# Differential attention on one Trainium2 core: sixteen value products of a tile split 7 and 9 between two score groups, in place of 3 and 13

## What is computed

```python
def block(args):
    qblk, qp = args                                   # 128 queries
    s = jnp.einsum('bqhce,bkhce->bchqk', qblk, k).astype(jnp.float32) * scale
    dist = jnp.abs(qp[:, None] - pos[None, :]).astype(jnp.float32)
    s = s - slopes[:, None, None] * dist
    a = jax.nn.softmax(s, axis=-1)
    w = a[:, 0] - lam * a[:, 1]
    return jnp.einsum('bhqk,bkhe->bqhe', w.astype(v.dtype), v)
```

## Time and profile before

| | |
|---|---|
| median of 3 runs | 2943.7 us (2941.12 to 2943.79) |
| the profiled execution | 2944.24 us, its span 2942.4 us |
| busy over the span | PE 2735.8 us (93%), PEld 2286.2 (78%), DVE 2032.5 (69%), ACT 1560.2 (53%), POOL 1054.5 (36%) |
| differential attention | 766 to 1296 us of the span |
| mean granted TensorE clock | 0.971 of full speed |

### The profile page before, as it was taken

One profiled execution on the slowest core, in us unless ns is written; L12 is line 12 of the kernel. 1 busy time (PEld: TensorE's weight loads), 2 busy tenths in 40 slices (PEclk: granted clock), 3 DMA queues, 4 the chain that ended last, 5 costly groups with the idle time before them and its releaser, 6 DMA issues. The chain is left out here.

```text
span 2942.4 us, 56410 instructions
## 1 busy us (share of the span) xinstructions
PE 2735.8 (93%) x22114; PEld 2286.2 (78%) x22114; DVE 2032.5 (69%) x2931; ACT 1560.2 (53%) x3111; POOL 1054.5 (36%) x803
## 2 busy tenths in 40 slices
PE   7899989999799999989998899899899999799998
PEld 5678867888588888879998678688677788577776
DVE  5767686666799999967776765433567766466675
ACT  6574446644588888867776221322433333455553
POOL 4677656777122222139550543200021011221211
PEclk9999999999899999999999899999999999799999
DMA  3433322332402120023443666242155466644441
GB/s 115 129 108 94 93 84 88 112 104 86 133 24 60 25 53 24 25 83 99 118 118 101 237 215 253 84 145 79 54 175 131 99 158 159 170 155 135 143 154 69
DMA packets 317445, 330.25 MB, mean 112 GB/s; under 512 B 24400, under 2 KB 259968, under 8 KB 314112
## 3 DMA queue, kind: packets, MB, share of 16 engines
q1 hardware_dynamic: 287184, 292.59, 32.7%
q0 software_dynamic: 6912, 23.07, 2.6%
q10 hardware_dynamic: 23088, 11.02, 1.6%
HBM read 217.13 MB, written 109.47 MB: 111 GB/s over the span
## 5 line engine op out<-in xcount | busy, mean ns | idle before, releaser
L1049 PE MATMUL p_acc<-p_y_hi,p_x_hi 128*128 128x512 f32 x904 | 363.2, 402 | 11.6 <-POOL p_x_lo L562 3.8
L1049 PE MATMUL p_acc<-p_y_lo,p_x_hi 128*128 128x512 f32 x904 | 357.1, 395 | 0.0
L1049 PE MATMUL p_acc<-p_y_hi,p_x_lo 128*128 128x512 f32 x904 | 357.1, 395 | 0.0
L562 POOL TENSOR_TENSOR p_x_lo<-k_carry,p_x_hi 128x1024 fp32r<-128x1024 f32 x113 | 281.9, 2501 | 133.8 <-ACT p_x_hi L634 133.8
L1894 ACT ACTIVATE d_e<-d_e,d_neg_top 128x2048 f32<-128x2048 f32 x128 | 256.8, 2006 | 18.8 <-DVE d_neg_top L1974 18.8
L2061 PEld LDWEIGHTS d_out<-d_v,d_w_t 64*128 64x128 f32 x4096 | 247.8, 188 | 11.9 <-ACT d_a_parts L1909 0.8
L920 DVE RECIPROCAL p_aux<-p_aux 128x512 f32<-128x512 f32 x64 | 215.1, 3361 | 55.8 <-ACT p_aux L730 55.8
L2061 PE MATMUL d_out<-d_v,d_w_t 64*128 64x128 f32 x4096 | 249.4, 272 | 0.7 <-ACT d_a_parts L1909 0.7
L1565 PE MATMUL s_acc<-s_y_hi,s_x_hi 128*128 128x512 f32 x560 | 223.5, 399 | 24.9 <-DVE s_x_lo L1369 13.0
L1565 PE MATMUL s_acc<-s_y_lo,s_x_hi 128*128 128x512 f32 x560 | 220.9, 395 | 0.0
L1565 PE MATMUL s_acc<-s_y_hi,s_x_lo 128*128 128x512 f32 x560 | 220.8, 394 | 0.0
(11 more groups left out here) (364 smaller groups left out, 7187.2 us busy)
## 6 DMA issues: line engine op xcount, KB each, us to landing
k_carry<-in_w_in SPq DMA_DIRECT2D x128, 256.0 KB, 3.3
k_carry<-in_a_w_in POOLq DMA_DIRECT2D x72, 256.0 KB, 3.6
cols<-p_z SPq DMA_DIRECT2D x64, 256.0 KB, 2.6
w_q<-q SPq DMA_DIRECT2D x15, 1024.0 KB, 7.6
o_parts<-l_stage SPq DMA_DIRECT2D x192, 66.0 KB, 1.9
m_o<-o_parts SPq DMA_DIRECT2D x48, 264.0 KB, 5.8
k_carry<-cols SPq DMA_DIRECT2D x48, 256.0 KB, 4.7
j_x_second<-x SPq DMA_DIRECT2D x20, 512.0 KB, 3.8
```

Of the source, the lines that this page charges most:

```text
L562: pool.tensor_tensor(x_lo[:, m % RING], inputs.place(x_place(m)), x_hi[:, m % RING].bitcast(F32), ALU.subtract).then_inc(x_lo_made, 1)
L1049: mm = pe.matmul(bank_of(n, j), x_part[:, n % RING, j, kt], y_part[:, y_slot(n), kt], start=(kt == 0 and m == 0 and not (g == 0 and n % 2 ...
```

## The change

One number in `diff_attention`, used only by TensorE's list:

```diff
@@ -1769,7 +1769,7 @@
             else:
                 eng.wait_ge(k_made, 2 * h)
 
-        EARLY = 3
+        EARLY = 7
         FILLED_AT = (11, 12, 15)
```

## The result

| | before | changed |
|---|---|---|
| median | 2942.41 us (4 runs, 2939.91 to 2943.79) | 2962.84 us (4 runs, 2959.2 to 2964.41) |
| ratio | | 1.0071, 95% interval 1.0056 to 1.0086 |
| profiled execution, span | 2944.24, 2942.4 us | 2962.72, 2960.9 us |

A forecast was written before the change was run, and what follows sets the result against it. The loop through ACT's copy was to bound the stage: 6.27 + 2.03 + 0.11 restart = 8.41 us a unit. Sixty periods +22.3, start -0.4, end -0.9, together +21.0, gave 2964.5 us, range 2955 to 2970.

The forecast's parts named there:

- The loop V, S10, D10, D11, E1, C, V: Per unit: first value product, third score group, DVE's third and fourth reads, second exponential, ACT's output copy, back; 8.41 us.
- S10 to D10: From the start of TensorE's third score group to DVE's third read of scores: 1.12 to 1.13 us.
- C to V: From ACT's copy of the previous unit's output to TensorE's first value product: 0.42 us, from a single sighting.
- D10 to D11: From DVE's third read of a unit's scores to its fourth: 1.40 us.
- The restart: Loss when value products resume after a wait: taken as 0.11 us, with bounds 0 and 0.16.
- V to T0: From the first value product to the first transpose group on TensorE: 1.56 us, or 1.67 with the restart.
- the lower end: Forecast with no loss at the restart of value products: period 8.30 us, total 2958 us.
- S11: TensorE's fourth score group of a unit; its wait for DVE was to be gone or nearly.
- Faster, by a shorter cycle: Rival: copy does not hold value products; TensorE and DVE loop over two units, 7.81 us each, 2929 us; chance 0.06.
- V to S10: From the first value product to the third score group on TensorE: 1.13 us before, 2.03 with the change.
- No change: Rival: the two effects cancel, period 7.95 to 8.15 us, total 2938 to 2949.6 us; chance 0.04.
- Slower still, by the clock: Rival: TensorE's longer idles lower its clock, one unit in ten costing 2.2 us more; 2978 us; chance 0.04.

The follow-up runs named there:

- e3_copy_late: Kernel before the change, with ACT's copy put behind the second pair of moves, no product moved; 2970.81 us, ratio 1.0099 to the kernel before.
- e7_copy_early: Changed kernel with ACT's copy put in front of the same step's second exponential; 2929.07 us, ratio 0.9953 to the kernel before.
- e8_copy_early: As e7_copy_early, but with eight key tiles in front of the first transposes; 2922.55 us, ratio 0.9937 to the kernel before.

## Why the prediction was right

- **The mechanism** was the forecast one. The loop V, S10, D10, D11, E1, C, V, hidden before, grew by the four moved tiles and became the longest. Two runs in which no product is moved switch its cost on and off by the place of the copy: on in the kernel before (e3_copy_late), off in the changed one (e7_copy_early).
- **Its size**: 8.38 in place of 8.41. S10 to D10 took 1.09, not 1.12 to 1.13; C to V took 0.41, not 0.42; D10 to D11 took 1.41, not 1.40. The restart was the unknown; V to T0 took 1.67, so it cost 0.11 as taken, not the 0 of the lower end (1.56).
- **The signs named**: V waiting some 60 times for 35 to 55 us (58 times, 39.3); D10 waiting 0.8 (0.81), S11 nearly none; ACT 1.4 before its moves and 0.2 before E1 (1.44 and 0.24); clock 1.00. All came. TensorE stood 0.66 us before V, where 0.74 were forecast.
- **The start** gained about 0.5 us, as expected: the first mixing comes at 780.07 before and at 779.66 in the changed kernel; with that 0.41 added, the first products of unit 1 come at 798.23 (797.82 in the trace) in place of 798.72.
- **The end** was wrong in sign. I took -0.9 us for the last two units and they cost more than before: from the first product of unit 61 to the last copy 15.2 us (1300.78 to 1315.99), against 14.5 (1281.00 to 1295.53). The step at fault is the one that priced 32 products at 0.1115 there. No scores are left to fill the wait for the copy, so TensorE stood still 2.11 us before unit 61, against 0.65 in the kernel before, and its clock fell (TensorE's timeline, then busy times with the clock in the third column from the end):

```profile
1300.78 2.81 PE L2061 MATMUL d_out<-d_v,d_w_t 64*128 64x128 f32 x28 [2.11 <-ACT d_a_parts L1909]
1303.37 1.07 PE L2044 MATMUL d_turn<-k_ident,d_e 64*128 64x64 f32 x16
```
```profile
1298.00:1301.00 3.00, 0.89 (x24) 0.75 (x22) 2.93 (x5) 2.76 (x6) 0.20 (x1) 1.00 0.00 0
1301.00:1303.00 2.00, 2.00 (x26) 2.00 (x26) 1.99 (x1) 0.70 (x2) 0.25 (x1) 0.60 0.15 41
1303.00:1305.00 2.00, 2.00 (x30) 2.00 (x30) 0.40 (x1) 0.52 (x2) 0.00 (x0) 0.54 0.00 0
```

  V to T0 took 2.59 there, against 1.67 in the loop. From V to T1, unit 61 took 5.80 us (1300.78 to 1306.58) and unit 62, at a clock of 1.00 again, 4.22 (1307.23 to 1311.45). These 1.58 us are the whole miss at the end. They and the 0.03 too much in each of 60 periods (1.8 us) cancelled; that the total came so close is in part luck.
- **A slip of words**: the prediction says that two transposed tiles of the first group stay behind S11. It is one tile, number 7, with its two products. Nothing hung on it.
- **The rivals.** 'Faster, by a shorter cycle' was the right loop for a kernel in which the copy does not hold V, as e7_copy_early and e8_copy_early showed; its condition, V to S10 under 1.68, was not met (2.14). The 1.68 gives a period of 7.95; for the 7.81 of that rival V to S10 would have had to be under 1.54. 'No change' wanted a period of 7.95 to 8.15, and it was 8.38. 'Slower still, by the clock' did not happen in the loop, where TensorE idles 0.66 us a unit at a clock of 1.00, but at the stage's end it did, once. What the Trainium skill says of idles between groups of matmuls (TensorE: Matmul & The Clock Gate, A second HAM failure mode: psum-queue depth-cycling) was so not seen for gaps of 0.66 us. The Trainium skill's advice for the gaps of the most contended engine, to let what blocks it start sooner (Perfetto Trace Analysis, Optimization Strategy), led to a gain here with one tile moved (-13.4 us) and to a loss with four (+20.4).

The stage from the first mixing to the last copy grew by 20.9 us (536.3 against 515.5); the profiled spans differ by 18.5. Of the 2.4 us between them, 0.4 lie ahead of the first mixing and 2.0 behind the last copy. The edit touches nothing there, and executions of one kernel differ by more (2939.91 to 2943.79 us before).

## What to carry over

When work is moved on an in-order engine into a gap, write down the loops that pass through the place it goes to, and not only the one it leaves: the first tile gained 0.22 us a unit, the second lost 0.10 and each of the next two 0.22 to 0.23, because a loop with 0.64 us of slack took over. A single sighting of a wait at the edge of a stage (here 0.42 us, and 0.11 for the restart) can be enough to price a loop that is hidden everywhere else. Before such a split is tuned, see which instruction on another engine closes the loop; putting the copy before a long exponential in place of behind it, together with a new split, gave more than any split alone that was tried. Four to six or more than eight tiles with the copy early were not run, so the best pair is not known.

## What was not expected of the hardware

- **POOL's add and DVE's mixing.** With the copy early, POOL's add of the two halves falls under DVE's mixing of two SBUF inputs (1007.71 to 1010.06), and took 2.19 us, where the median in the kernel before is 0.46 (e7_copy_early):

```profile
1008.18 2.19 POOL L1851 TENSOR_TENSOR d_a_out<-d_a_parts 128x128 f32<-128x128 f32 x1 [5.82 <-ACT d_a_parts L1909]
```
```profile
1007.71 2.35 DVE L1994 SCALAR_TENSOR_TENSOR d_e<-d_e,d_ratio 128x2048 f32<-128x2048 f32 x1
```

  It ended 0.31 us after the mixing, which kept its 2.35 us. So it was in 61 of 64 units of each run with the copy early: the add ended 0.30 to 0.33 us after the mixing, whether it had begun 0.5 or 2.0 us before the mixing's end. The Trainium skill (SBUF — State Buffer, Who interferes with whom) names the pair of ports that the two engines share as a lock, not a shared rate; the trace agrees. The 0.31 us behind the mixing are less than the 0.46 the add takes alone; no run shows what part of it was done before. ACT's squaring, which waits for this add, came only at 1014.91.
- **The restart after a wait.** A first value product behind a wait is followed by the next ones 0.11 us later than in a stream, also where the profile puts the wait on its weight load alone (five tiles in front). A score group loses nearly nothing (0.80 against 0.78).
- **The clock at the stage's end.** Some 2.1 us without matmuls were followed by a stretch at a granted clock of 0.60 and 0.54, against 1.00 with gaps of 0.66 us in every unit.
